# Two-layer decoder step on one core: paired heads' compressed exp, layer norm on token rows, and another order for the last block and the final norm

## What is computed

```python
# layer 0: chunk_gmlp
z = gelu(h @ w_in); u, v = split(z)
v = layernorm(v, ln_g, ln_b)                       # over the 1024 features; v is also an output
mixed = einsum('gts,bcsge->bctge', w_s * causal, vc) + b_s.T[:, :, None]
out = (u * mixed) @ w_out
# layer 1: nsa_layer, for each head
p_c = masked_softmax(s_c - slopes * d_c)           # compressed branch, 15 blocks
p_s, p_w = ...                                     # selected and window branches
out = g0 * (p_c @ vc) + g1 * (p_s @ v_sel) + g2 * (p_w @ vw)
# end: expert outputs weighted, added to x, then
y = x * rsqrt(mean(x * x) + eps) * norm_final
```

## Time and profile before

| | |
|---|---|
| runs | 1315.2, 1307.4, 1304.76 us; median 1307.4 |
| profiled execution | 1308.13 us, of which the span from first to last instruction is 1306.5 |
| busy, share of span | PE 95%, PE weight load 81%, DVE 80%, ACT 71%, POOL 6% |
| mean granted PE clock | 0.981 |
| HBM traffic | 367.41 MB read, 27.45 MB written, 302 GB/s over the span |

### The profile page before, as it was taken

One profiled execution on the slowest core, in us unless ns is written; L12 is line 12 of the kernel. 1 busy time (PEld: TensorE's weight loads), 2 busy tenths in 40 slices (PEclk: granted clock), 3 DMA queues, 4 the chain that ended last, 5 costly groups with the idle time before them and its releaser, 6 DMA issues.

```text
span 1306.5 us, 21438 instructions
## 1 busy us (share of the span) xinstructions
PE 1245.1 (95%) x7272; PEld 1061.8 (81%) x7272; DVE 1045.3 (80%) x1462; ACT 928.2 (71%) x1378; POOL 77.1 (6%) x77
## 2 busy tenths in 40 slices
PE   6889999999998789999999999999999999999996
PEld 6879999999965667788888888888888888887874
DVE  6777766567527955998998997998998998989985
ACT  5655454456465984987987887888888879868863
POOL 1000000004201001100000000000000000003400
PEclk9999999999997988999999999999999999999998
DMA  8474445557569535998998998998998998998920
GB/s 347 161 257 171 172 179 194 194 194 255 157 227 389 201 151 207 403 422 343 402 407 325 410 405 319 414 396 328 415 391 329 417 389 331 420 377 328 409 118 34
DMA packets 59711, 391.50 MB, mean 300 GB/s; under 512 B 6686, under 2 KB 12962, under 8 KB 21186
## 3 DMA queue, kind: packets, MB, share of 16 engines
q1 hardware_dynamic: 51010, 354.29, 69.0%
q0 software_dynamic: 8640, 36.40, 7.5%
HBM read 367.41 MB, written 27.45 MB: 302 GB/s over the span
## 4 chain that ended last, share of the span: by engine, by line
PE 78%; DVE 9%; ACT 7%; issue 4%; DMA 2%; DVEq 0%; ACTq 0%; SPq 0%
PE bank L1853 17%; PE bank L1855 16%; PE bank L1854 16%; PE bank L1481 7%; PE bank L1482 7%; PE bank L1483 7%; DVE w_lo L1363 3%; DMA ring<-in_wd 2%; ACT arena L754 2%; PE bank L1838 1%; DVE d_lo L967 1%; ACT arena L718 1%; ACT slc_v L761 1%; ACT w_hi L829 1%; DVE total L942 1%
## 5 line engine op out<-in xcount | busy, mean ns | idle before, releaser
L1363 DVE TENSOR_TENSOR w_lo<-raw,w_hi 128x1024 fp32r<-128x1024 f32 x528 | 623.0, 1221 | 35.8 <-ACT w_hi L829 18.3
L829 ACT CAST w_hi<-raw 128x1024 fp32r<-128x1024 f32 x528 | 543.0, 1055 | 93.5 <-PE bank L1855 92.5
L1853 PE MATMUL bank<-w_hi,xg_hi 128*128 128x512 f32 x704 | 275.0, 391 | 1.5 <-DVE w_lo L1363 1.5
L1855 PE MATMUL bank<-w_hi,xg_lo 128*128 128x512 f32 x704 | 274.4, 390 | 0.0
L1854 PE MATMUL bank<-w_lo,xg_hi 128*128 128x512 f32 x704 | 274.0, 389 | 0.0
L967 DVE TENSOR_TENSOR d_lo<-ring,d_hi 128x1024 fp32r<-128x1024 f32 x120 | 148.2, 1240 | 87.4 <-ACT d_hi L602 87.3
L1481 PE MATMUL bank<-hA_hi,d_hi 128*128 128x264 f32 x640 | 185.3, 290 | 11.7 <-DVE hA_lo L957 8.9
L1482 PE MATMUL bank<-hA_lo,d_hi 128*128 128x264 f32 x640 | 183.1, 286 | 0.0
L1483 PE MATMUL bank<-hA_hi,d_lo 128*128 128x264 f32 x640 | 182.8, 286 | 0.0
L602 ACT CAST d_hi<-ring 128x1024 fp32r<-128x1024 f32 x120 | 125.0, 1045 | 75.7 <-PE bank L1483 66.3
L1853 PEld LDWEIGHTS bank<-w_hi,xg_hi 128*128 128x128 f32 x704 | 132.0, 188 | 29.4 <-DVE w_lo L1363 2.2
(11 more groups left out here) (310 smaller groups left out, 1485.6 us busy)
## 6 DMA issues: line engine op xcount, KB each, us to landing
raw<-in_moe SPq DMA_DIRECT2D x264, 1024.0 KB, 6.8
ring<-in_wd SPq DMA_DIRECT2D x29, 2048.0 KB, 8.5
out_rows<-zeros POOLq DMA_DIRECT2D x1, 6656.0 KB, 39.7
slot_rows<-zeros POOLq DMA_DIRECT2D x1, 6144.0 KB, 26.4
out_rows<-yrow POOLq DMA_DIRECT2D x8, 512.0 KB, 7.6
xs<-slot_rows POOLq DMA_DIRECT2D x7, 512.0 KB, 3.5
arena<-in_cmp_pages POOLq DMA_DIRECT2D x16, 128.0 KB, 3.4
X2v<-in_cmp_pages POOLq DMA_DIRECT2D x16, 128.0 KB, 2.6
```

What stands on the lines that cost most here:

```text
L829: nc.scalar.copy(w_hi[:, i % NSPLIT, :], raw[:, u % NRAW, ITEM * (i % 2):ITEM * (i % 2) + ITEM])\
L1363: V.tensor_tensor(w_lo[:, i % NSPLIT, :], raw[:, (i // 2) % NRAW, ITEM * (i % 2):ITEM * (i % 2) + ITEM], w_hi[:, i % NSPLIT, :].bitcast(F3 ...
L1853: T.matmul(out, lhs_hi, hi, start=first, stop=False)
L1855: return T.matmul(out, lhs_lo, hi, start=False, stop=last)
```

## The change

1. **Layer norm.** The sums over chunks, both `mean_of` calls, the subtraction, the squares and the wide reciprocal are gone. PE transposes the gelu'd v behind products 8, 9 and 10 (`VT` gives each its pair of banks), ACT copies it to `vtok` with a row sum and squares it with a row sum, DVE normalises the rows without gain and bias (`normed_rows`). Gain and bias go into the spatial stage: PE multiplies `ones` with the masked spatial weights, DVE puts bias times these sums into `b_s` (`mixed_bias`), and L1031 becomes a product with the gain plus `b_s`. For the output v, PE transposes the normed rows back behind products ao 0 to 3, and ACT applies gain and bias.
2. **Attention.** The two 15-column branches of both heads of a pair share one exp, without row sum; DVE subtracts their maxima first and sums them later. `scores(0)` goes ahead of the compressed values and of `sample_scores(1)`; on DVE `biased_max(0)` leads, and `sample_max`, `sample_scale`, `sample_turned` come later; on PE `sample_turn` stands behind `scores(2)`.
3. **End.** Weighting and summing of the rows gathered back go from slices 6 to 8 into 7 to 9; `add_back` from slices 9 and 10 to slice 10 and the two gaps between the last down products. ACT copies the left half of the last rows, DVE the right. The combining uses five banks. Squares are added in pairs, and PE takes the mean of four pairs per token, the root and reciprocal are taken on 3 columns, PE spreads them, DVE multiplies, four stores.

```diff
                 act.wait_ge(v_scaled, c + 1)
                 nc.scalar.activation(vT[:, c, :], vT[:, c, :], ACT.Gelu_apprx_tanh).then_inc(v_ready, 1)
+            spread = []
+
+            def rows_in_tokens(t):
+                r = P if t < 2 else NS
+                for half in range(2):
+                    act.wait_ge(vt_done, 2 * t + half + 1)
+                    nc.scalar.activation(vtok[0:r, t, 512 * half:512 * half + 512], VT[t][half][0:r, :], ACT.Copy,
+                                         accum_out=st[0:r, 2 * t + half:2 * t + half + 1]).then_inc(vt_ready, 1)
+
+            def spread_of(t):
+                r = P if t < 2 else NS
+                act.wait_ge(ln_mu, t + 1)
+                out = (hB[:] if t < 2 else sqr).rearrange("p k t -> p (k t)")[0:r, (t % 2) * DM:(t % 2) * DM + DM]
+                spread.append(nc.scalar.activation(out, vtok[0:r, t, :], ACT.Square,
+                                                   bias=st[0:r, 9 + t:10 + t], accum_out=st[0:r, 12 + t:13 + t]))
+
...
+                if c < 3:
+                    rows_in_tokens(c)
+                if 2 <= c < 5:
+                    spread_of(c - 2)
+                    settle(spread[-1])
+                    nc.scalar.activation(st[:, 15:18], st[:, 12:15], ACT.Sqrt, scale=1.0 / DM, bias=vector("eps")[:, 1:2]).then_inc(std_ready, 1)
...
+                if c < 4:
+                    for k in (2 * c, 2 * c + 1):
+                        act.wait_ge(vt_done, 7 + k)
+                        nc.scalar.activation(vT[:, k, :], (T0, T1)[k % 2][:, 0:NT], ACT.Identity, bias=vector("lnb")[:, k:k + 1],
+                                             scale=vector("lng")[:, k:k + 1]).then_inc(vn_ready, 1)
...
+                for j, (a, z) in enumerate([(0, 128), (414, 542), (128, 384), (542, 798)]):
                     ins = nc.scalar.activation(S[:, a:z], S[:, a:z], ACT.Exp, bias=mx[:, b, j:j + 1],
                                                accum_out=sm[:, b, j:j + 1])
+                if i % 2 == 0:
+                    act.wait_ge(neg_max, 2 * (i // 2) + 2)
+                    ins = nc.scalar.activation(Sh[:, b:b + 2, 384:414], Sh[:, b:b + 2, 384:414], ACT.Exp)
                 ins.then_inc(exps, 1)
...
             exp_head(0)
             exp_head(1)
+            sample_exp()
             exp_head(2)
...
+            act.wait_ge(left_done, 1)
+            act.wait_ge(yrow_free, last + 2)
+            nc.scalar.copy(yrow[:, 0:512], B[2][:, :]).then_inc(left_ready, 1)
+            root_table()
...
-                if k:
-                    add_up(vT, k - 1, v_ready, k)
-            add_up(vT, KC - 1, v_ready, KC)
...
+                r = P if t < 2 else NS
+                dve.wait_ge(vt_ready, 2 * t + 2)
+                settle(V.tensor_tensor(st[0:r, 6 + t:7 + t], st[0:r, 2 * t:2 * t + 1], st[0:r, 2 * t + 1:2 * t + 2], ALU.add))
+                V.tensor_scalar(st[0:r, 9 + t:10 + t], st[0:r, 6 + t:7 + t], -1.0 / DM, None, ALU.mult).then_inc(ln_mu, 1)
+
+            def normed_rows():
+                nstd[0] += 1
+                dve.wait_ge(std_ready, nstd[0])
+                settle(V.reciprocal(st[:, 15:18], st[:, 15:18]))
+                for t in range(3):
+                    r = P if t < 2 else NS
+                    V.tensor_scalar(vtok[0:r, t, :], vtok[0:r, t, :], st[0:r, 9 + t:10 + t], st[0:r, 15 + t:16 + t], ALU.add, ALU.mult)\
+                        .then_inc(z_ready, 1)
+
+            def mixed_bias():
+                dve.wait_ge(sums_done, 1)
+                for g in range(8):
+                    both = b_s[:, g, 0:NP].rearrange("p (t n) -> p t n", n=P)
+                    sums = (STAT, MISC)[g // 4][:, (g % 4) * P:(g % 4 + 1) * P].unsqueeze(1).to_broadcast([P, 2, P])
+                    V.scalar_tensor_tensor(both, sums, vector("lnb")[:, g:g + 1], both, ALU.mult, ALU.add)
+                settle(V.tensor_tensor(st[:, 18:26], vector("w00"), vector("lnb"), ALU.mult))
+                settle(V.tensor_tensor(b_s[:, :, NP:NT], b_s[:, :, NP:NT], st[:, 18:26].unsqueeze(2).to_broadcast([P, 8, NS]), ALU.add))
...
+                if 1 <= c < 4:
+                    token_means(c - 1)
+                if c == 5:
+                    normed_rows()
+                if c == 6:
+                    mixed_bias()
...
-                    V.tensor_tensor(hB[:, g, :], b_s[:, g, :], B[g % 4][:, 0:NT], ALU.add).then_inc(mixed, 1)
+                    V.scalar_tensor_tensor(hB[:, g, :], B[g % 4][:, 0:NT], vector("lng")[:, g:g + 1], b_s[:, g, :], ALU.mult, ALU.add)\
+                        .then_inc(mixed, 1)
...
+                dve.wait_ge(neg_max, 2 * p + 1)
+                cmp_ = both[:, :, 384:414].rearrange("p x (t n) -> p x t n", n=NCMP)
+                V.tensor_tensor(cmp_, cmp_, mx[:, b:b + 2, 4:6].unsqueeze(3).to_broadcast([P, 2, 2, NCMP]), ALU.add).then_inc(neg_max, 1)
...
+                cmp_ = both[:, :, 384:414].rearrange("p x (t n) -> p x t n", n=NCMP)
+                settle(V.tensor_reduce(sm[:, b:b + 2, 4:6], cmp_, AX_X, ALU.add))
...
+            biased_max(0)
+            compressed_values()
             sample_max()
-            biased_max(0)
+            biased_max(1)
             sample_scale()
-            biased_max(1)
+            scale(0)
             sample_turned()
-            scale(0)
...
+                bank = LAST_BANKS[c] if n else (STAT, MISC)[c % 2]
...
+                    if ends and 7 <= f < 10:
+                        back_summed(f - 7)
+                    if ends and f == FT - 1:
+                        for c in range(4):
                             add_combined(0, c)
...
-            for c in range(KC + 1):
-                if c < KC:
-                    add_combined(1, c)
-                if c:
-                    add_up(sq_last, c - 1, sq_ready, 32 + c)
-            inv_std()
-            normed(late("final"))
+            for c in range(4, KC):
+                add_combined(0, c)
+            dve.wait_ge(item_used, last * ITEMS + ITEMS + NSPLIT)
+            dve.wait_ge(yrow_free, last + 2)
+            V.tensor_copy(yrow[:, 512:1024], B[3][:, :]).then_inc(right_ready, 1)
+            for c in range(KC):
+                add_combined(1, c)
+                if c in (2, 4, 6, 7):
+                    j = c // 2 - 1 if c < 7 else 3
+                    dve.wait_ge(sq_ready, 32 + 2 * j + 2)
+                    V.tensor_tensor(sq_last[:, 2 * j, :], sq_last[:, 2 * j, :], sq_last[:, 2 * j + 1, :], ALU.add).then_inc(sum_step, 1)
+            dve.wait_ge(tok_std, 2)
+            V.reciprocal(tok_rstd[:, 0:2], tok_rstd[:, 0:2]).then_inc(tok_scale, 1)
+            V.reciprocal(tok_rstd[0:NS, 2:3], tok_rstd[0:NS, 2:3]).then_inc(tok_scale, 1)
+            dve.wait_ge(rstd_spread, 1)
+            for k in range(KC):
+                V.scalar_tensor_tensor(hB[:, k, :], x[:, k, :], late("final")[:, k:k + 1], MISC[:, 0:NT], ALU.mult, ALU.mult)\
+                    .then_inc(h_ready, 1)
...
-                if c == 8:
-                    mean_of()
-                if c == 11:
-                    mean_of()
...
+                if 8 <= c < 11:
+                    t = c - 8
+                    a, z = ((0, P), (P, NP), (NP, NT))[t]
+                    if t == 0:
+                        pe.wait_ge(spatial_in, 48)
+                        pe.wait_ge(v_ready, KC)
+                    if t == 2:
+                        pe.wait_ge(vt_ready, 2)
+                    for half, bank in enumerate(VT[t]):
+                        for k in range(4):
+                            i = T.transpose(bank[0:z - a, k * P:(k + 1) * P], vT[:, 4 * half + k, a:z], ident)
+                        i.then_inc(vt_done, 1)
+                if c == 12:
+                    pe.wait_ge(ws_ready, 2)
+                    pe.wait_ge(vt_ready, 4)
+                    for half, bank in enumerate((STAT, MISC)):
+                        i = T.matmul(bank[:, :], const("ones"), wsT[:, 4 * half:4 * half + 4, :], start=True, stop=True)
+                    i.then_inc(sums_done, 1)
...
+                if c < 4:
+                    for k in (2 * c, 2 * c + 1):
+                        if k >= 2:
+                            pe.wait_ge(vn_ready, k - 1)
+                        for t, (a, z) in enumerate([(0, P), (P, NP), (NP, NT)]):
+                            i = T.transpose((T0, T1)[k % 2][:, a:z], vtok[0:z - a, t, k * P:(k + 1) * P], ident[0:z - a, 0:z - a])
+                        i.then_inc(vt_done, 1)
...
+            pe.wait_ge(pre_ready, 2)
+            pe.wait_ge(cmp2_ready, 1)
+            scores(0)
+
...
+            pe.wait_ge(gtok_ready, 2)
+            sample_scores(1, "WK")
+            for c in range(2):
+                i = T.matmul(STAT[:, PAST + NS:PAST + NS + NS * NCMP], Qc[:, c, :], kcT[:, 8 * c:8 * c + 8, :], start=(c == 0), stop=(c == 1))
+            i.then_inc(ss_done, 1)
...
-            scores(0)
             scores(1)
-            pe.wait_ge(cmp2_ready, 2)
-            sample_turn()
```

(33 more changed lines are left out.)

160 lines of the change are left out of this document (50 added, 110 removed).

## The result

| | before | after |
|---|---|---|
| first median, on which the forecast stands | 1307.4 us (3 runs) | |
| median of all runs | 1314.1 us (16 runs, 1301.3 to 1317.0) | 1302.4 us (16 runs, 1299.9 to 1305.4) |
| ratio after to before | | 0.9918 (95%: 0.9901 to 0.9936) |
| profiled execution: time, span | 1308.13, 1306.5 us | 1302.13, 1300.5 us |

The change makes the kernel 0.8% faster: 0.0082 of 1314.1 is 10.8 us (8.4 to 13.0), where 13.2 was forecast. The absolute time, 1302.4, lies 8.2 above the 1294.2 of the forecast and 1.4 above its range. Of the 8.2, 6.7 are the old kernel's own: its median of three was 1307.4, that of sixteen is 1314.1. The other 1.5 are gain that did not come (13.2 less the 11.7 between the two medians; the ratio says 10.8). So two questions are open: why the old kernel's executions differ by 16 us and the new one's by 5.5, and which terms of the sum hold.

The account below looks back on a forecast made before the run. PE bounds the kernel, running without gaps between three places; in the attention loop ACT leads, with DVE close. Layer norm 3.3, attention 2.8 and last block and end 7.1 sum to 13.2, taking 1307.4 to 1294.2 us; range 1288.5 to 1301.

Parts of the forecast that it names:

- Slower: Feed-forward: the later window-state copy delays weight tiles; fair sharing a wait of 3, copy served first 1311; chance 0.04.
- The rule of turns by packet: Copy beside weight tiles: each DMA engine alternates between its queues packet by packet, so the copy is not served first throughout.
- Layer norm: Start to feed-forward: loop over g starts at 70.1, 24 back-transposes cost 2.8; net gain 3.3, between 1.0 and 4.5.
- the price of 0.115 apiece: Back-transposes behind products ao 0 to 3: 24 priced at 2.8 us from eight measured in 0.92.
- Attention: Attention loop gains 2.6 with DVE as the new limit, its start 0.2; together 2.8, between 0 and 5.5.
- the lower bound of -2.0: Attention's start: PE at its lower clock for all 64 matmuls of the samples' values; the term was net 0.2.
- The last block and the end: Stall before `add_back` goes, 4.0; shorter work behind the last matmul, 3.1; together 7.1.
- one of under 1: Last block: sign that the end is right, a PE gap of under 1 before the last down product, none near 1262.
- The two with a smaller gain: Rivals: samples late, attention gives 0, 1297 (0.18); layer norm gives nothing, gain 0 to 1, 1297 (0.14).
- The samples come late: Attention's start: sample values run slowly, the loop's first maxima start 2 later, attention gives 0, 1297; chance 0.18.
- 0.45 faster, 0.51 within 1%: Whole kernel: chance 0.45 of over 1% faster, 0.51 of within 1%, 0.04 of over 1% slower.

Follow-up runs that it names:

- Kernels with spare products: Useless extra PE products put into PE's gaps: old kernel with three 0.9946; kernel after, window-state copy issued early, with five 0.9873, with two 0.9856.
- the last kernel: Kernel after with the window-state copy early, two spare products in the spatial part and three in each of three gaps at the attention's start: 1294.0 us, 0.9862.

## Why the prediction was wrong, point by point

The profiles of all kernels give the length of each stage; the means are over the executions with the old and the new form of that stage.

| Stage | forecast gain | old form, executions | new form, executions | difference |
|---|---|---|---|---|
| start to 25th dense item | 3.3 | 106.68 (101.4 to 109.8, 6) | 103.13 (102.5 to 103.6, 4) | 3.55 |
| 25th to 29th dense item | 0 | 12.40 (all others) | 17.79 (copy late and in large packets, 2) | -5.39 |
| 29th dense to first expert item | 2.8 | 396.33 (394.5 to 398.2, 5) | 393.18 (392.5 to 393.7, 7) | 3.15 |
| first expert item to last expert matmul | 4.0 | 775.87 (775.3 to 776.9, 6) | 770.94 (770.5 to 771.4, 8) | 4.93 |
| last expert matmul to the end | 3.1 | 18.27 (18.1 to 18.6, 6) | 16.04 (15.5 to 16.6, 8) | 2.23 |

Kernels with spare products are left out of the first row, and the paired exp alone and the last kernel out of the third. Each number is one profiled execution's, and the kernels of a row differ elsewhere; the last row's new form has two values, 15.5 and 16.6, and with the second TensorE is at the lower clock for 11.8 us at the end instead of 7.9. The sum is 8.5, at the lower end of the measured 8.4 to 13.0; four of the five terms are within 1 us of the forecast.

**The step that failed is the one that priced the moved copy at nothing.** The prediction named the mechanism among its rivals, and even its moderate price: "a tile takes at most twice as long, 18, a wait of 3". The tile took 17.4 and PE stood for 3.58. But this stood inside the rival "Slower", beside an extreme in which two late tiles had to cost some 17 us (1311 against 1294), and got 0.04; in the sum the moved copy was worth 0. (The extreme itself does not bear out what was put on it: 1311 is 0.3% above 1307.4, not over 1%.) Two mistakes led there. The rule of turns by packet was read as a rule of equal shares, without looking at the packets: by turns, 64 KB against 16 KB gives the copy four times the tile's bytes, as measured from 110 us on, and before that the tile got nothing for 6 us. And a moderate outcome of a rival belongs into the sum as a term with a price, also when its extreme is improbable. With that term, 3.3 + 2.8 + 7.1 - 5.4, the forecast had been 7.8.

With the copy early, the median of 1297.9 lies inside the range.

**The base was the second, and of the 8.2 us by which the time was missed it is the larger part, 6.7.** The sum was made against one profiled execution and a median of three, and the earlier trace rows showed the clock of its stretches only where I asked for it. Of the 16 us by which the old kernel's executions differ, some 7 are decided in one place by the clock, and the profiled execution was of the quicker kind. The prediction set the clock's cost where the trace showed it (1265.7 to 1271.1) and nowhere else; that the same gaps of 2.4, 0.7 and 0.7 could cost 7 us in the next execution was not weighed, though the three times shown, 1304.8, 1307.4 and 1315.2, asked for it. In the gain the two errors worked against each other. Most executions of the old kernel are of the slower kind, whose start to the 25th item takes 109.0 (four traces): against those the first row is 5.8, and the rows add up to 5.8 - 5.4 + 3.2 + 4.9 + 2.2 = 10.7, beside the 10.8 measured. That the gain came within 2.4 of the 13.2 is luck.

**Layer norm.** The DVE steps came as worked out: `normed_rows` 2.4 for 2.3, `mixed_bias` 3.2 for 3.0, loop over g at 70.25 for 70.1. Wrong were two things that the profile shows plainly. The spatial part ran wholly at the lower clock, behind a gap of 2.22 before 69.71 for which the prediction had no term (PE waits for the last u chunk, which DVE scales only after `mixed_bias`); with the clock kept up the first addition to x comes at 81.6 instead of 83.5, 5.5 before the old kernel's, where 6.1 was forecast. And the 24 back-transposes cost 4 times 1.09, 4.4, instead of 2.8 (two output products are 3.99 apart with six of them between, 2.90 without): the price of 0.115 apiece was taken from eight in a row on one operand, and six between two products cost 0.18 each. That those two losses still leave 3.55 on average, close to the 3.3, is chance: the old layer norm's own clock loses more. In the two traces at hand they leave -0.8, and with the full clock on both sides, as above, -2.2: in these traces the new layer norm is no gain of its own, it only loses less to the lower clock than the old form usually does.

**Attention.** Right in the mechanism of the loop: DVE takes over as the limit (28.6 of 29.4 busy), and a pair takes 7.35 where DVE's sum gave 7.27. Against the rounding of the 29th item, the first exp of pair 7 came 3.2 earlier in the two traces: 1.8 of it in the loop, for 2.3, and 1.4 at its start, for 0.2. The samples came late in the way that the rival feared and the lower bound of -2.0 was put on: their values ran at the lower clock (the first three groups of 16 in 1.94, 1.96 and 1.96, where the old kernel had 1.93, 1.49 and 1.04), and one of their scalings still stood for 1.64 under POOL's fill. The loop began earlier nevertheless, so that price was wrong. Alone the attention measured 5.0 (2.1 to 7.8) for 2.8.

**The last block and the end.** 4.9 for 4.0, and 2.2 for 3.1 (3.2 between the two traces at hand): 7.2 for 7.1 together. (The items named for the end add up to 2.9, not 3.1: 1.2, 0.4, 1.05 and 0.26.) The stall went, the new waits are 0.48 and 0.38, as "one of under 1" had it; alone it measured 4.9 (2.4 to 7.5).

**Rivals.** None of the four is what happened. The two with a smaller gain stood for other causes; "Slower" had the right cause at the wrong size. *The samples come late* met its condition and not its price. The expectation "0.45 faster, 0.51 within 1%" is not contradicted by 0.8%.

Open is why the clock falls in most executions of the old kernel and not in some: the gaps are equal to 0.1 us, only the time at which they fall differs, by 1.8, and no run here sets that time on its own.

## What to carry to other kernels

When a change moves a DMA in time, ask what else uses the DMA engines at its new place, and compare the packet sizes, not only the bytes: a large contiguous copy takes turns in 64 KB packets and leaves a stream of 16 KB packets a fifth of the bytes while both run, and here nothing for 6 us before that, and cutting it smaller or issuing it in a quiet stretch gives the time back. Before one profiled execution becomes the base of a sum, look whether its time is typical of the runs, and look at the granted clock of every stretch behind a gap: short gaps in front of thin matmuls can cost several times their length, and a spare product or two in the gap is the cheapest test of it, and here the cheapest cure. Try it on the old form before a rewrite is credited with the gain.

## What the runs showed of the hardware that was not expected

- Gaps of 2.4, 0.7 and 0.7 us around thin transposes left TensorE at 1.2 GHz for 3.4 us in one execution of the same code and for 23.9 in another, although PE was busy for 22.5 of the 24 us from 69 on (at the lower clock its work takes longer). With 2 us of spare products in the first of them the clock stayed at 2.4 GHz.
- Two DMA queues on the same engines went packet for packet while both had packets under way: 16 of 65.5 KB against 16 of 16.4 KB (1.05 and 0.26 MB), and 84 of 3.8 KB against 83 of 16.4 KB (0.32 and 1.36 MB). Other sizes were not tried.
- A tile issued while the copy was running got its first packet late: 6.4 us after its issue behind 65.5 KB packets, 3.6 behind 4 KB ones, 1.0 without the copy. So the packet size is not the whole of that wait.
- Six transposes between two dense products (four of 128 rows, two of 8) cost 1.09 us, while eight of 128 columns in a row cost 0.92.
